# Transposing the raw input before its norm is known, and applying the norm's row to the results

## The reference

```python
def rms_norm(x, w):
    xf = x.astype(jnp.float32)
    y = xf * lax.rsqrt(jnp.mean(xf * xf, axis=-1, keepdims=True) + EPS)
    return (y * w.astype(jnp.float32)).astype(x.dtype)
...
u = rms_norm(h, ln_pre_mix[i])
proj = u @ w_in[i]
q_a, k_a, v_a, qkv_b, z_b, b_b, a_b, gate_a, gate_b = jnp.split(proj, IN_SPLITS, axis=-1)
qa = apply_rope(to_heads(q_a, N_HEADS_MOBA), cos, sin)
ka = apply_rope(to_heads(k_a, N_HEADS_MOBA), cos, sin)
qkv_b = jax.nn.silu(causal_depthwise_conv(qkv_b, conv_w[i]))
```

## Time and profile before

| | us |
|---|---|
| time, median of 3 runs (966.02 to 968.13) | 966.08 |
| the profiled execution | 965.95 |
| its span, first to last instruction | 964.1 |
| TensorE busy | 951.5 (99%) |
| GpSimd busy | 743.0 (77%) |
| ScalarE busy | 498.1 (52%) |
| VectorE busy | 367.5 (38%) |

### The profile page before, as it was taken

How to read it: one execution, slowest core, us unless ns; L and a number is a source line. 1 busy time by engine, 2 the same in 40 slices (tenths; PEclk the granted TensorE clock), 3 DMA queues, 4 the chain that set the end, 5 groups by cost and what they waited for, 6 DMA issues and landing times.

```text
span 964.1 us, 14578 instructions
## 1 busy us (share of the span) xinstructions
PE 951.5 (99%) x5652; PEld 808.6 (84%) x5652; DVE 367.5 (38%) x865; ACT 498.1 (52%) x727; POOL 743.0 (77%) x593
## 2 busy tenths in 40 slices
PE   9999999999999999999999999999999999999997
PEld 8978879988788888888888887899888888888885
DVE  5676626785526244121123245062342341111103
ACT  5564625454544357545454566584565564444431
POOL 5968654876746988799877987868876889888890
PEclk9999999999999999999999999999999999999999
DMA  8736342655434766777654675645564567666541
GB/s 262 215 115 198 106 135 85 178 163 164 132 110 138 252 216 179 236 196 205 187 157 150 217 219 169 239 146 183 175 202 149 154 179 213 190 182 192 177 131 44
DMA packets 76749, 167.31 MB, mean 174 GB/s; under 512 B 8349, under 2 KB 13705, under 8 KB 76553
## 3 DMA queue, kind: packets, MB, share of 16 engines
q1 hardware_dynamic: 71296, 156.40, 53.2%
q10 hardware_dynamic: 5384, 9.99, 3.1%
HBM read 165.32 MB, written 1.05 MB: 173 GB/s over the span
## 4 chain that ended last, share of the span: by engine, by line
PE 93%; DVE 4%; ACT 1%; issue 1%; DMA 0%; DVEq 0%; ACTq 0%
PE L L515 22%; PE L L517 22%; PE L L516 21%; PE Q L515 2%; PE Q L517 2%; PE Q L516 2%; PE L L887 1%; PE L L889 1%; PE L L888 1%; PE Q L732 1%; PE Q L1172 1%; PE L L786 1%; PE L L788 1%; PE L L787 1%; PE Q L850 1%; PE L L825 1%
## 5 line engine op out<-in xcount | busy, mean ns | idle before, releaser
L502 POOL TENSOR_TENSOR w_lo<-raw,w_hi 128x512 fp32r<-128x512 f32 x588 | 741.6, 1300 | 197.5 <-ACT w_hi L1320 197.1
L1320 ACT CAST w_hi<-raw 128x1024 fp32r<-128x1024 f32 x294 | 305.1, 1054 | 257.5 <-PE L L517 120.8
L515 PE MATMUL L<-w_hi,uH 128*128 128x512 f32 (+1 forms) x768 | 304.9, 397 | 0.3
L517 PE MATMUL L<-w_hi,uL 128*128 128x512 f32 (+1 forms) x768 | 296.4, 386 | 0.0
L516 PE MATMUL L<-w_lo,uH 128*128 128x512 f32 (+1 forms) x768 | 295.9, 385 | 0.0
L515 PEld LDWEIGHTS L<-w_hi,uH 128*128 128x128 f32 x768 | 144.4, 188 | 29.6 <-DVE uL L1921 1.5
L517 PEld LDWEIGHTS L<-w_hi,uL 128*128 128x128 f32 x768 | 144.3, 188 | 29.6
L516 PEld LDWEIGHTS L<-w_lo,uH 128*128 128x128 f32 x768 | 144.6, 188 | 26.7 <-issue 0.5
L515 PE MATMUL L<-w_hi,hH 128*128 128x512 f32 x176 | 69.0, 392 | 0.0
L517 PE MATMUL L<-w_hi,hL 128*128 128x512 f32 x176 | 68.6, 390 | 0.0
L516 PE MATMUL L<-w_lo,hH 128*128 128x512 f32 x176 | 68.5, 389 | 0.0
(11 more groups left out here) (359 smaller groups left out, 1257.7 us busy)
## 6 DMA issues: line engine op xcount, KB each, us to landing
raw<-in_w_in SPq DMA_DIRECT2D x88, 512.0 KB, 3.7
raw<-in_w_ffn_gate SPq DMA_DIRECT2D x22, 512.0 KB, 3.7
raw<-in_w_ffn_up SPq DMA_DIRECT2D x22, 512.0 KB, 3.6
raw<-in_w_ffn_down SPq DMA_DIRECT2D x22, 512.0 KB, 3.5
raw<-in_w_gate SPq DMA_DIRECT2D x22, 512.0 KB, 3.7
raw<-in_w_up SPq DMA_DIRECT2D x22, 512.0 KB, 3.7
raw<-in_w_down SPq DMA_DIRECT2D x22, 512.0 KB, 3.5
raw<-in_w_out SPq DMA_DIRECT2D x16, 512.0 KB, 3.6
```

The source lines that it names most:

```text
L502: last = nc.gpsimd.tensor_tensor(lo[:, cc], raw[:, n % RAW, cc], hi[:, cc].bitcast(F32), ALU.subtract)
L515: mm(dst, sH, wH, start=start, stop=False)
L517: return mm(dst, sL, wH, start=False, stop=stop)
L1320: copy(halves[SLOT[u]][0], raw[:, u % RAW, :]).then_inc(w_hi_there, 1)
```

## The change

x is transposed as it lands, without its root: `xn0` is no longer made. The roots come later on VectorE. TensorE spreads them over a 128x256 row (`rows0`, every partition holds the root of each token) by two matmuls at the end of conv(0,0), and VectorE copies that row to SBUF. Whoever reads a result of `uH`/`uL` now multiplies: VectorE the conv banks and `baT` by the row, ScalarE the tables `cos1`/`sin1` (four 128x128 instructions in rates, which scale the rotated queries and keys), and the values, z, ga and gb by a scale argument of an instruction that was there. Besides, `warm(15)` becomes `warm(7)` and `warm(5)` goes; unit 0 is cast in two halves, the first with a mark of its own; the second low half of unit 3 is made by VectorE; and the load of `table` (740 KB) moves behind the cast of unit 3.

```diff
@@ SyncE, GpSimd
+                if n == 3 + RAW:
+                    sp.wait_ge(*VE(("u",), "last low"))
...
-                for half in range(2):
+                for half in range(1 if n == 3 else 2):
@@ TensorE, first_conv
-                    pe.wait_ge(w_hi_there, n0 + j + 1)
                     for k in (2 * j, 2 * j + 1):
+                        if k == 0:
+                            pe.wait_ge(*AC(("u",), "first slice"))
+                        else:
+                            pe.wait_ge(w_hi_there, n0 + j + 1)
...
+                    if j == 3:
+                        pe.wait_ge(*VE(("u",), "last low"))
...
+                for t in range(NT):
+                    pe.wait_ge(*VE(("u",), "root", t))
+                    last = mm(Q[1][:, t * P:(t + 1) * P], rstd0[:, t:t + 1].to_broadcast([P, P]), ident, start=True, stop=True)
+                last.then_inc(*PE.mark(("u",), "rows"))
@@ TensorE, u
-                    warm(15)
+                    warm(7)
...
-                    warm(5)
-                    for t in range(NT):
+                    for t in range(NT):
+                        pe.wait_ge(landed[f"x{t}"], 16)
...
@@ ScalarE, u
-                    load("table", table[:, P:], a["table"][:, P:])
...
+                    act.wait_ge(w_landed[0], 16)
+                    copy(halves[SLOT[0]][0][:, 0:512], raw[:, 0, 0:512]).then_inc(*AC.mark(step, "first slice"))
+                    copy(halves[SLOT[0]][0][:, 512:UNIT], raw[:, 0, 512:UNIT]).then_inc(w_hi_there, 1)
+                    made[0] = 1
+                    act.wait_ge(*VE(step, "taps"))
...
+                    load("table", table[:, P:], a["table"][:, P:])
                 elif kind == "rates":
                     split_up_to(consumed + SPLIT + 1)
+                    act.wait_ge(landed["table"], 16)
+                    act.wait_ge(*VE(("u",), "root", 1))
+                    for t in range(NT):
+                        actf(cos1[:, t, :], cos1[:, t, :], ACT.Copy, scale=rstd0[:, t:t + 1])
+                        last = actf(sin1[:, t, :], sin1[:, t, :], ACT.Copy, scale=rstd0[:, t:t + 1])
+                    last.then_inc(*AC.mark(step, "rotation"))
                     act.wait_ge(*VE(step, "ba"))
@@ ScalarE, values, z, ga, gb: scale=rstd0[:, t:t + 1] added
@@ VectorE, u: roots and scaling of x taken from the front; behind the last uL
+                    dve.wait_ge(*AC(step, "ss", 1))
+                    for t in range(NT):
+                        ts(rv[:, t:t + 1], ss[:, t:t + 1], 1.0 / D, EPS, ALU.mult, ALU.add)
+                        rsqrt_one(rstd0[:, t:t + 1], rv[:, t:t + 1], step, "root", t)
+                    dve.wait_ge(w_hi_there, 4)
+                    hi, lo = halves[SLOT[3]]
+                    tt(lo[:, UNIT // 2:], raw[:, 3, UNIT // 2:], hi[:, UNIT // 2:].bitcast(F32), ALU.subtract, step, "last low")
                     dve.wait_ge(landed["ba"], 16)
...
+                    dve.wait_ge(*PE(step, "rows"))
+                    v(V.tensor_copy(rows0, Q[1][:, 0:SEQ]))
@@ VectorE, conv
+                        if (gr, part) == (0, 0):
+                            tt(src, src, rows0, ALU.mult)
+                        elif ct % 2 == 0:
+                            both = (Q[2 + ct // 2] if (gr, part) == (0, 1) else L[2 * (part % 2) + ct // 2])[:].rearrange("p (a n) -> p a n", a=2)
+                            tt(both, both, each(rows0, 2), ALU.mult)
                         ts(dst, src, cwv[:, 3, tile:tile + 1], None, ALU.mult, None)
```

More of the change, by code:

```diff
@@ L271, in build @@
         table = place("table", [P, 5 * P + 2 * NT * HD + ROPE2 + LEVELS * HALF])
-        small = place("small", [P, 960])
+        small = place("small", [P, 960 + SEQ])
         at[0] += (base - at[0]) % SPAN
@@ L376, in tiny @@
             free[0] += n
-            assert free[0] <= 960
+            assert free[0] <= 960 + SEQ
             return small[:, free[0] - n:free[0]]
@@ L418, in build @@
         r1, floor = tiny(8), tiny(8)
+        rows0 = tiny(SEQ)
         baH = big("baH", 36, [P, KD, 16], F32R)
@@ L934, in _ @@
                     pe.wait_ge(*VE(step, "constant"))
-                    warm(15)
+                    warm(7)
                     pe.wait_ge(landed["ident"], 16)
-                    pe.wait_ge(landed["cwr"], 16)
-                    pe.wait_ge(landed["ln0"], 16)
-                    turn(L[3][:, 0:n], cwr[0:n, :], ident[0:n, 0:n]).then_inc(*PE.mark(step, "taps"))
-                    warm(5)
                     for t in range(NT):
+                        pe.wait_ge(landed[f"x{t}"], 16)
                         for j in range(4):
-                            pe.wait_ge(*(VE(step, "scaled", 1, j) if t == 1 and j < 2 else AC(step, "scaled", t, j // 2)))
                             for i in range(2):
-                                last = turn(Q[j][:, i * SEQ + t * P:i * SEQ + (t + 1) * P], xn0[:, t, (2 * j + i) * P:(2 * j + i + 1) * P], ident)
+                                last = turn(Q[j][:, i * SEQ + t * P:i * SEQ + (t + 1) * P], x0[:, t, (2 * j + i) * P:(2 * j + i + 1) * P], ident)
                             if t == 1:
                                 last.then_inc(*PE.mark(step, "turned", j))
+                        if t == 0:
+                            pe.wait_ge(landed["cwr"], 16)
+                            pe.wait_ge(landed["ln0"], 16)
+                            turn(L[3][:, 0:n], cwr[0:n, :], ident[0:n, 0:n]).then_inc(*PE.mark(step, "taps"))
                 elif step in INSIDE:
@@ L1542, in _ @@
                             act.wait_ge(*PE(("att", 0), "out", 1))
+                        act.wait_ge(*VE(("u",), "root", 1))
                         for t in range(NT):
-                            copy(mtok[:, 2, t, :, :], L[2 + t][:].rearrange("p (h d) -> p h d", h=GH)).then_inc(*AC.mark(step, "v", t))
+                            actf(mtok[:, 2, t, :, :], L[2 + t][:].rearrange("p (h d) -> p h d", h=GH), ACT.Copy, scale=rstd0[:, t:t + 1]).then_inc(*AC.mark(step, "v", t))
                 elif kind == "feat":
@@ L1580, in _ @@
                     for t in range(NT):
-                        last = actf(dst[:, t, c * 512:(c + 1) * 512], L[banks[t]][:], fn)
+                        last = actf(dst[:, t, c * 512:(c + 1) * 512], L[banks[t]][:], fn, scale=rstd0[:, t:t + 1])
                     last.then_inc(*AC.mark(step))
@@ L1998, in roped @@
                     dve.wait_ge(*fed(step))
+                    dve.wait_ge(*AC(("rates",), "rotation"))
                     if gr == 1 and part == 0:
@@ L2022, in _ @@
                     v(V.memset(C[:, 0, :], 1.0), step, "constant")
-                    for t in range(NT):
[L2024 to L2032, removed]
+                    dve.wait_ge(*PE(step, "taps"))
+                    v(V.tensor_copy(cw, L[3][:, 0:CONV * 24 + KD]), step, "taps")
                     for j in range(4):
@@ L2048, in _ @@
                     tt(baL[:], bv, baH[:].bitcast(F32), ALU.subtract, step, "split")
+                    dve.wait_ge(*PE(step, "rows"))
+                    v(V.tensor_copy(rows0, Q[1][:, 0:SEQ]))
                 elif kind == "ba":
                     dve.wait_ge(*PE(step))
-                    v(V.tensor_copy(baT[0:16, :], Q[0][0:16, 0:SEQ]), step, "turned")
+                    tt(baT[0:16, :], Q[0][0:16, 0:SEQ], rows0[0:16, :], ALU.mult, step, "turned")
                 elif kind == "rates":
```

## The result

The changed kernel takes 967.98 us (median of 20 runs, 967.61 to 970.21) against 966.01 us before (20 runs, 965.77 to 969.59): 1.0016 times, with a 95% interval of 1.0009 to 1.0024. It is slower by less than 0.3%, where the prediction said 968.4. The profiled execution has a span of 965.8 us instead of 964.1.

The account below looks back on a forecast made before the run. TensorE bounds the kernel, with VectorE's chain ending its waits at tok. -2.14 + 0.27 + 0.45 + 0.1 + 1.0 + 1.47 + 1.13 = +2.28 takes the span from 964.1 to 966.4, the time to 968.4 us; range 966.6 to 970.9.

Parts of the forecast that it names:

- Start, taken off: First conv(0,0) matmul at 9.1 us instead of 11.24, waiting only for unit 0's landing and half a cast: -2.14 us.
- it lands 6.8 us after its issue: Unit 0's transfer at the start: issued at about 1.64 us, so landing at 8.44.
- Start, given back: First matmul to ba: wait for unit 1's cast +0.27, the row's two matmuls +0.45, VectorE's low half +0.1 us.
- just hidden: Ahead of ba: VectorE's low half, then baH and baL, end at 21.5 us; ba asks at 21.4; +0.1.
- Scalings: ScalarE's four 128x128 scalings in rates, ahead of the sigmoid's table load: 0.25 us each, +1.0.
- Multiplications: VectorE's two by the row per conv: conv(0,2) +1.47 us, conv(1,2) +1.13, conv(0,1) and conv(1,1) hidden.
- Waits: TensorE at tok: about 3.6 and 1.9 us in group 0, a new one of about 1.1 for kdec in group 1.
- The clock was up at the first conv: Rival: the clock falls, first conv's matmuls 0.24 us apart instead of 0.12; 970.0 us, chance 0.28.
- The low half was not late: Rival: VectorE's chain of roots, low half, baH, baL slips by 0.8 us and TensorE waits; 969.2 us, chance 0.12.
- group 1 had no more slack than reckoned: Rival: group 1's chain has more room than 0.34 and 0.1 us, or scalings hide under the cast; 967.2, chance 0.1.
- the multiplications reached TensorE: Rival: multiplications reach nobody, TensorE's two waits were not for this chain, only the start counts; 964.8 us, chance 0.05.
- the early start came: Rival: no early start, unit 0 lands later or transposes wait for the taps' transfers; +1 to +2 us, chance 0.05.

## Why the prediction was right, point by point

- **Start, taken off (-2.14).** The mechanism held: cast of half a unit, then the first matmul 0.69 behind the landing (0.67 was reckoned). The size did not: the earlier trace rows is one landing, 8.42, of a transfer that lands at 7.35 to 8.43. The step "it lands 6.8 us after its issue" took one execution for the rule; the middle of the traces is 7.7 to 7.8, the first matmul 8.4 to 8.5, so -2.8 and not -2.14.
- **Start, given back (+0.27, +0.45, +0.1).** From the first matmul to ba 12.41 was reckoned and 12.51 measured. Within it the wait for unit 1's cast was 0.2, the row 0.60 instead of 0.45, and the low half took 1.20 instead of 1.57 but `baH` 1.21 instead of 0.23. `baL` ended at 20.63 and ba started at 20.69: the prediction's "just hidden" is about what the rows show.
- **Scalings (+1.0).** 1.15 by experiment. ScalarE's 128x128 instructions took 0.39 and followed each other by 0.30; 0.25 was taken.
- **Multiplications.** conv(0,2) +1.46 (1.47 reckoned), conv(0,1) 0.0 (0), under the table load that was named as its cover; conv(1,2) +1.13 (1.13), conv(1,1) nothing, as said, though read from the trace and not tested.
- **Waits.** 3.56 and 1.89 at tok of group 0 (3.6 and 1.9), 0.96 in group 1 (about 1.1). That the 3.56 split into two places was not foreseen: the fill of moba(0,1) needs conv(0,2)'s banks, which before were free (61.26) ahead of TensorE.
- **Sum.** With the middle of the start's gain, -1.9, and +1.15, +1.46, +1.13, it is +1.8; the medians say +1.97. The prediction's +2.28 was too high by the start (0.6), and too low by the scalings (0.15). Three steps of the account it did not have at all: +0.15 at 152, -0.6 at 302 and +0.5 at 316 to 323. That they add up to 0.05 is luck.
- **Rivals.** The clock was up at the first conv. That had luck in it too: in the latest of the traces it came up at 7.62, 0.5 us ahead of the first matmul at 8.14, and nothing in the prediction secured this margin. The low half was not late, group 1 had no more slack than reckoned, the multiplications reached TensorE, and the early start came.

## What to carry to other kernels

A gain upstream of a wait is not a gain: it lengthens the wait, unless the chain that ends it starts from the same place and gets nothing new. Before moving work onto such a chain, ask what in it could run beside something else; here three table loads and a product stood behind work they did not need, and reordering them took the changed kernel from 968.0 to 961.6 us, 0.5% under the kernel before, three times the 2.0 us that the change had lost. And where a start is to hang on a transfer or on the clock, take its time from several executions.

## What the runs showed of the hardware

**VectorE and GpSimd take turns.** In the start of the changed kernel VectorE's three instructions with SBUF inputs took 1.20, 1.21 and 1.27 us (rows above); GpSimd's at that time ended at 17.55, 19.24 and 20.49, one of them taking 1.74 instead of 1.29:

```profile
16.26 2.98 POOL L505 TENSOR_TENSOR w_lo<-raw,w_hi 128x512 fp32r<-128x512 f32 x2
```

VectorE's end at 18.09, 19.33 and 20.64, each 0.1 to 0.5 us behind one of those. This fits VectorE being held until GpSimd's instruction ends, and GpSimd's next one being held in turn while VectorE finishes (the 1.74). With the load of the tables in its old place the same low half of 128x512 began when GpSimd had only 0.32 us left, not 0.66, and took 0.87 us instead of 1.20. The same cast of `baH` took 0.23 us before, where it began 0.09 ahead of GpSimd's instruction, and 0.73 in the run with GpSimd's low half, ending 0.08 behind one:

```profile
16.34 0.23 DVE L2047 CAST baH<-small 128x128 fp32r<-128x128 f32 x1
```
```profile
17.39 0.73 DVE L2057 CAST baH<-small 128x128 fp32r<-128x128 f32 x1
```

The Trainium skill, SBUF — State Buffer, section Who interferes with whom, calls it an exclusive lock held for an instruction, won by whoever issues first. The traces agree. An estimate of the price from them: an instruction's own time (0.54 and 0.55 us for that low half in the two runs, 0.1 to 0.2 for the cast) plus what is left of GpSimd's.

**A dip of the clock.** In one of the traces (GpSimd's low half) TensorE's granted clock was 0.50 from 76 to 79.3, some 1.3 us after its wait for `kdec` ended: its lower level, and the matmuls came 0.43 us apart instead of 0.23; 1.6 us were lost. No other trace has a dip at this wait, which nine of them have at the same length (1.87 to 1.89 us), so the wait alone does not bring it; what does stays open.

```profile
76.00:79.00 3.00, 3.00 (x9) 0.50 0.62 190
80.00:82.00 2.00, 2.00 (x10) 1.00 0.61 162
```
